# A two-block kernel on one Trainium2 core: the first block's mixer steps regrouped by ScalarE table set

## The reference, cut to what matters

```python
# gated delta rule: q, k, v are projected, convolved (4 taps) and passed through Silu
qkv = jax.nn.silu(causal_depthwise_conv(jnp.concatenate([q, k, v], axis=-1), conv_w))
q, k, v = jnp.split(qkv, 3, axis=-1)
q = l2norm(to_chunks(q, DN_HEADS, DN_DHEAD)) * (DN_DHEAD ** -0.5)
k = l2norm(to_chunks(k, DN_HEADS, DN_DHEAD))
M = jnp.where(strict, beta * (k @ k.T) * decay, 0.0)     # by chunk of 64 tokens
T = inverse(eye + M);  u0 = T @ (beta * v);  wk = T @ (beta * exp(G) * k)
qk = (q @ k.T) * decay
# a scan over the 8 chunks with u0, wk, qk, then per head:
o = rmsnorm(o, norm_g) * jax.nn.silu(z)

# HGRN2
fg = lb + (1.0 - lb) * jax.nn.sigmoid(f)
qc, kc, Bc = jax.nn.silu(q), 1.0 - fg, jnp.cumsum(jnp.log(fg))
# ... a scan over chunks, then:  o = rmsnorm(o, norm_g) * jax.nn.silu(g)

# second block, forgetting attention
fq = _rms(_to_heads(fx_q, FOX_HEADS)) * g_qk[0]
fk = _rms(_to_heads(fx_k, FOX_HEADS)) * g_qk[1]
```

## Time and profile before

| | |
|---|---|
| time, median of 3 runs | 3634.67 us (3631.44 to 3637.55) |
| the profiled execution: its own time | 3640.12 us |
| its span | 3638.4 us, TensorE's granted clock 0.985 of full |
| PE busy | 3562.5 us (98%) |
| VectorE busy | 1975.6 us (54%) |
| ScalarE busy | 1596.9 us (44%) |
| DMA | 368.21 MB, 101 GB/s |

### The profile page before, as it was taken

One profiled execution on the slowest core, in us unless ns is written; L12 is line 12 of the kernel. 1 busy time (PEld: TensorE's weight loads), 2 busy tenths in 40 slices (PEclk: granted clock), 3 DMA queues, 4 the chain that ended last, 5 costly groups with the idle time before them and its releaser, 6 DMA issues.

```text
span 3638.4 us, 50031 instructions
## 1 busy us (share of the span) xinstructions
PE 3562.5 (98%) x20724; PEld 2984.6 (82%) x20724; DVE 1975.6 (54%) x3335; ACT 1596.9 (44%) x2472; POOL 111.5 (3%) x202
## 2 busy tenths in 40 slices
PE   9999999999999999999999979999999999889999
PEld 7887988887887888898888758888888887678888
DVE  6966577548773677454445555444533345553332
ACT  7457444336655534242223694322332237843221
POOL 0000100010000100010000100000000000000000
PEclk9999999999999999999999999999999999999999
DMA  3101244431201244434443211444332321112232
GB/s 125 65 31 41 88 153 148 154 129 65 65 24 58 93 149 152 153 98 159 147 148 125 68 49 45 157 156 148 130 104 96 95 91 59 47 54 92 99 99 86
DMA packets 108690, 368.21 MB, mean 101 GB/s; under 512 B 14129, under 2 KB 16561, under 8 KB 108465
## 3 DMA queue, kind: packets, MB, share of 16 engines
q1 hardware_dynamic: 108464, 365.02, 30.1%
HBM read 360.78 MB, written 4.19 MB: 100 GB/s over the span
## 4 chain that ended last, share of the span: by engine, by line
PE 86%; ACT 7%; DVE 5%; issue 1%; POOL 0%; DMA 0%; SPq 0%; DVEq 0%; ACTq 0%; POOLq 0%
PE bank L175 84%; ACT L400 3%; ACT tmp L190 1%; PE bank L259 1%; DVE score L217 1%; DVE ast L214 1%; ACT wh L190 1%; PE bank L181 1%; DVE wl L193 1%; DVE tmp L196 0%; ACT lr L190 0%; ACT hh L190 0%; DVE dv L196 0%; ACT fl L190 0%; ACT lu L190 0%
## 5 line engine op out<-in xcount | busy, mean ns | idle before, releaser
L175 PE MATMUL bank<-hh,wh 128*128 128x512 f32 (+2 forms) x3424 | 1290.9, 377 | 18.3 <-ACT lg L190 13.0
L175 PE MATMUL bank<-hh,wl 128*128 128x512 f32 (+2 forms) x3424 | 1284.8, 375 | 0.7 <-DVE wl L193 0.7
L175 PE MATMUL bank<-hl,wh 128*128 128x512 f32 (+2 forms) x3424 | 1285.3, 375 | 0.0
L190 ACT ACTIVATE wh<-raw 128x1024 fp32r<-128x1024 f32 (+1 forms) x542 | 559.4, 1036 | 1449.0 <-PE bank L175 1443.8
L193 DVE TENSOR_TENSOR wl<-raw,wh 128x1024 fp32r<-128x1024 f32 (+1 forms) x542 | 646.7, 1196 | 843.1 <-ACT wh L190 842.9
L175 PEld LDWEIGHTS bank<-hh,wh 128*128 128x128 f32 (+1 forms) x3424 | 648.7, 189 | 138.7 <-issue 28.8
L175 PEld LDWEIGHTS bank<-hh,wl 128*128 128x128 f32 (+1 forms) x3424 | 648.2, 189 | 114.1 <-issue 5.6
L175 PEld LDWEIGHTS bank<-hl,wh 128*128 128x128 f32 (+1 forms) x3424 | 648.7, 189 | 111.8 <-issue 6.5
L175 PE MATMUL bank<-ah,wh 128*128 128x512 f32 (+1 forms) x1188 | 437.1, 368 | 0.0
L175 PE MATMUL bank<-ah,wl 128*128 128x512 f32 (+1 forms) x1188 | 437.0, 368 | 0.0
L175 PE MATMUL bank<-al,wh 128*128 128x512 f32 (+1 forms) x1188 | 436.4, 367 | 0.0
(11 more groups left out here) (353 smaller groups left out, 3551.6 us busy)
## 6 DMA issues: line engine op xcount, KB each, us to landing
raw<-in_up_dram SPq DMA_DIRECT2D x264, 512.0 KB, 3.3
raw<-in_ada_dram SPq DMA_DIRECT2D x144, 512.0 KB, 4.3
raw<-in_in_dram SPq DMA_DIRECT2D x88, 512.0 KB, 3.3
raw<-in_down_dram SPq DMA_DIRECT2D x96, 448.0 KB, 3.3
raw<-in_down_dram SPq DMA_DIRECT2D x48, 512.0 KB, 3.5
raw<-in_out_dram SPq DMA_DIRECT2D x32, 512.0 KB, 3.3
x<-in_x_dram SPq DMA_DIRECT2D x16, 256.0 KB, 5.2
raw<-in_in2v_dram SPq DMA_DIRECT2D x8, 512.0 KB, 3.5
```

Source lines behind the costliest of these rows:

```text
L175: s = self.put(lambda e: e.matmul(out, lhsT, rhs, **kw), records * max(records * n, 2 * m) / 2.4)
L190: return self.put(lambda e: e.activation(out, x, func, **kw), cost, tables)
```

## The change

Three things are edited. The Ln of `head_rstd` no longer asks for the set `natural_log`, so it takes the set that holds both Ln and Exp. `dn_project` is split into `conv` (project, taps, Silu) and `unit` (the norm), and runs k0 k1, their norms, then q0 q1 v0 v1, then the norms of q. `hg_project` runs the Sigmoids of both f tiles, then the Ln, scan and Exp of both, then the Silus of q0 q1 g0 g1. The planner's distance for a near step becomes a parameter; no section sets it, and its default is 5.2e3 where it was 4 x 1300.

```diff
-DEFAULT = dict(slack=(20e3, 100e3), part=0.5, more=3e3, stay=5e3, busy=20.0, goal=3.7e3)
+DEFAULT = dict(slack=(20e3, 100e3), part=0.5, more=3e3, stay=5e3, busy=20.0, goal=3.7e3, near=5.2e3)
...
-            near = [r for r in ready[e] if (not steps[r[1]].tables or table in steps[r[1]].tables) and r[0] < pick[0] + 4 * switch]
+            near = [r for r in ready[e] if (not steps[r[1]].tables or table in steps[r[1]].tables) and r[0] < pick[0] + way["near"]]
...
-    log = q.act.activation(t.ap[:, :], b.ap[:, :], ACT.Ln, bias=mem.eps[:, 0:1], scale=1.0 / n, table="natural_log").then_inc(q.act.sem, 1)
+    log = q.act.activation(t.ap[:, :], b.ap[:, :], ACT.Ln, bias=mem.eps[:, 0:1], scale=1.0 / n).then_inc(q.act.sem, 1)
...
     def dn_project(p):
         q, v, d = mem.lane("dn_in"), mem.pairs[p], {}
-        for kind, dst in enumerate((v.q, v.k, v.v)):
-            for e in range(2):
...
+        def conv(kind, e):
+            u = 4 * kind + 2 * p + e
+            b, done = project(u)
...
+            d[kind, e] = q.act.activation(y, y, ACT.Silu).then_inc(q.act.sem, 1)
+
+        def unit(kind, e):
+            y, t, b = to[kind][:, e, :], in_tmp.next(), prep.next()
+            m = sum_squares(mem, q, y, d[kind, e], mem.k("ones"), b, t)
...
+        for kinds, normal in (((1,), 1), ((0, 2), 0)):
+            for kind in kinds:
+                for e in range(2):
+                    conv(kind, e)
             for e in range(2):
...
+                unit(normal, e)
         return d
...
     def hg_project(wait):
-        q, d, tmp = mem.lane("hg_in"), {}, Turn(tmps[2:4])
-        for i in range(2):
-            b, done = project(22 + i)
-            q.act.wait_ge(done, wait)
-            d["q", i] = q.act.activation(mem.hq[:, i, :], b.ap[:, :], ACT.Silu).then_inc(q.act.sem, 1)
...
+        q, d, ts = mem.lane("hg_in"), {}, tmps[2:4]
+        for i, t in enumerate(ts):
             b, done = project(24 + i)
...
+        for i, t in enumerate(ts):
             rest, minus, least = (x[:, i:i + 1] for x in mem.bounds[l])
...
-            b, done = project(26 + i)
-            q.act.wait_ge(done, wait)
-            d["g", i] = q.act.activation(mem.hg[:, i, :], b.ap[:, :], ACT.Silu).then_inc(q.act.sem, 1)
...
+        for name, to, u in (("q", mem.hq, 22), ("g", mem.hg, 26)):
+            for i in range(2):
+                b, done = project(u + i)
+                q.act.wait_ge(done, wait)
+                d[name, i] = q.act.activation(to[:, i, :], b.ap[:, :], ACT.Silu).then_inc(q.act.sem, 1)
```

More of the change, by code:

```diff
@@ new lines, in dn_project @@
+        to = v.q, v.k, v.v
+        def conv(kind, e):
+            u = 4 * kind + 2 * p + e
+            b, done = project(u)
+            w = lambda k: mem.p1(l, "conv", 12 * k + u)
+            y = to[kind][:, e, :]
+            q.act.wait_ge(done)
+            s = q.act.activation(y, b.ap[:, :], ACT.Copy, scale=w(3)).then_inc(q.act.sem, 1)
+            for k in (2, 1, 0):
+                z = 3 - k
+                q.dve.wait_ge(s)
+                s = q.dve.scalar_tensor_tensor(to[kind][:, e, z:], b.ap[:, 0:S - z], w(k), to[kind][:, e, z:], ALU.mult, ALU.add).then_inc(q.dve.sem, 1)
+            b.free = [s]
+            q.act.wait_ge(s)
+            d[kind, e] = q.act.activation(y, y, ACT.Silu).then_inc(q.act.sem, 1)
@@ new lines, in unit @@
+        def unit(kind, e):
+            y, t, b = to[kind][:, e, :], in_tmp.next(), prep.next()
+            m = sum_squares(mem, q, y, d[kind, e], mem.k("ones"), b, t)
+            q.act.wait_ge(m)
+            log = q.act.activation(t.ap[:, :], b.ap[:, :], ACT.Ln, bias=mem.eps[:, 0:1]).then_inc(q.act.sem, 1)
+            b.free = [log]
+            q.act.wait_ge(log)
+            inverse = q.act.activation(t.ap[:, :], t.ap[:, :], ACT.Exp, scale=-0.5, bias=mem.eps[:, 1:2] if kind == 0 else None).then_inc(q.act.sem, 1)
+            q.dve.wait_ge(inverse, d[kind, e])
+            d[kind, e] = q.dve.tensor_tensor(y, y, t.ap[:, :], ALU.mult).then_inc(q.dve.sem, 1)
+            t.free = [d[kind, e]]
@@ L1838, in hg_project @@
     def hg_project(wait):
-        q, d, tmp = mem.lane("hg_in"), {}, Turn(tmps[2:4])
-        for i in range(2):
-            b, done = project(22 + i)
-            q.act.wait_ge(done, wait)
-            d["q", i] = q.act.activation(mem.hq[:, i, :], b.ap[:, :], ACT.Silu).then_inc(q.act.sem, 1)
-            b.free = [d["q", i]]
+        q, d, ts = mem.lane("hg_in"), {}, tmps[2:4]
+        for i, t in enumerate(ts):
             b, done = project(24 + i)
-            t = tmp.next()
             q.act.wait_ge(done, t.free, wait)
-            s = q.act.activation(t.ap[:, :], b.ap[:, :], ACT.Sigmoid).then_inc(q.act.sem, 1)
-            b.free = [s]
+            d["k", i] = q.act.activation(t.ap[:, :], b.ap[:, :], ACT.Sigmoid).then_inc(q.act.sem, 1)
+            b.free = [d["k", i]]
+        for i, t in enumerate(ts):
             rest, minus, least = (x[:, i:i + 1] for x in mem.bounds[l])
-            q.dve.wait_ge(s, mem.bounds_ready, wait)
+            q.dve.wait_ge(d["k", i], mem.bounds_ready, wait)
             d["k", i] = q.dve.tensor_scalar(mem.hk[:, i, :], t.ap[:, :], minus, rest, ALU.mult, ALU.add).then_inc(q.dve.sem, 1)
@@ L1862, in hg_project @@
             d["gl", i] = q.pool.memset(mem.hgl[:, i, 0:1], 0.0).then_inc(q.pool.sem, 1)
-            b, done = project(26 + i)
-            q.act.wait_ge(done, wait)
-            d["g", i] = q.act.activation(mem.hg[:, i, :], b.ap[:, :], ACT.Silu).then_inc(q.act.sem, 1)
-            b.free = [d["g", i]]
+        for name, to, u in (("q", mem.hq, 22), ("g", mem.hg, 26)):
[3 more added lines that the diff above has]
+                d[name, i] = q.act.activation(to[:, i, :], b.ap[:, :], ACT.Silu).then_inc(q.act.sem, 1)
+                b.free = [d[name, i]]
         d["i"] = []
```

## The result

The changed kernel takes 3613.9 us (median of 4 runs, 3613.7 to 3616.5), the kernel before 3633.1 (4 runs, the three above among them): a ratio of 0.9949, 95% interval 0.9932 to 0.9966. Run again later beside others it took 3614.4 us, ratio 0.9940 (0.9926 to 0.9953). So the change makes the kernel faster by half a per cent, some 19 us; 3620 was predicted.

A forecast was written before the change was run, and what follows sets the result against it. TensorE was taken as full in the first block's long stretches, leaving gains in the mixers' ends: -7.7, -4.5 and -2.0 make -14.2 us, 3620.5 against the median of 3634.67. Predicted 3620 us, range 3602 to 3643.

The forecast's parts named there:

- The bound: First block's long mixer stretches: TensorE is full, so fewer loads there gain 0; at most some 4 us.
- Number of loads: Whole kernel: table loads fall from 192 to about 125, by 39, 20 and 8 for the three edits.
- Layer 2's end: End of first block's layer 2 mixer: six loads go where TensorE waits for ScalarE, -7.7 us; bounds 0 and -15.3.
- VectorE's half of each head: Layer 2's end: named as what is late next after the loads, but with room, busy 12.01 of 24 us.
- rival 1: Mixers' ends: another wait takes the loads' place, or loads don't fall; nothing gained, 3633 us; chance 0.18.
- Layer 1's end: End of first block's layer 1 mixer: head norm loads go, TensorE gives back its filler, -4.5 us; bounds 0 and -5.6.
- Second block: Its mixers: 8 loads a layer go, hidden under TensorE; -2 us over both layers; bounds -9.6 and +2.6 a layer.
- The delta rule's loop: Second pair, first block: loop starts 25.4 us later as q comes later; 0 in both layers, bound +7 in layer 1.
- rival 2: Delta rule: v1 still projected late, so q's norm and loop wait; slower, 3645 us, if v1's Copy passes 1045; chance 0.14.
- the slack: Layer 2, second pair: 29.1 us between the loop's end and u0, which takes in the loop's delay.
- Rival 3: Full stretches and second block: TensorE less full than it looks, so shorter ScalarE chains pay there too; 3600 us; chance 0.14.

The follow-up runs named there:

- b1: The kernel before, unchanged, run for a second profile: span 3628.5 us, first block's mixer of layer 1 396.61 us at a granted clock of 1.00.
- again: The changed kernel itself, run once more for a further profile: 3614.4 us, ratio 0.9940 to the kernel before.
- e1: The kernel before with only the head norms' Ln moved to the set of Ln and Exp, planned anew: 3622.1 us, ratio 0.9969.
- e2: The kernel before with only the delta rule's projection regrouped: ratio 1.0002, 172 loads.
- e3: The kernel before with only the HGRN2 projection regrouped: ratio 1.0006, 183 loads.
- e5: The kernel before, every engine's list in its old order, loads worked out anew with head norms' Ln in the shared set: 3623.3 us, ratio 0.9970.
- e9: The changed kernel with only the second block's head norms on a set of their own again, planned for: 3619.6 us, ratio 0.9963 to the kernel before.
- e8: The changed kernel with the LRU's root by Ln and Exp and the second block's planner told to stay on a loaded set: 3609.0 us, ratio 0.9932.
- e6: The changed kernel in its own order, with a separate set loaded again for each head norm, unplanned: 3656.2 us, ratio 1.0054 to the kernel before.
- b2: The kernel before, unchanged, run for a third profile: first block's mixer of layer 1 400.42 us at a granted clock of 0.99.

## Why the prediction was right, point by point

The sum, -14.2, stands against -15.2 between two executions at like clock (b1 and `again`) and -19 by the medians. Part of that nearness is luck: the terms missed in both directions.

*The bound.* PE full in the first block's long stretches: right. (The 3% of the chain are a rounded share, so 109 us is no upper bound, as the prediction has it; 3.5% would be 127. Nothing rests on it.) Regrouping by itself gave 1.0002 and 1.0006. From the mixer's start to the last z Silu the changed kernel is 2.2 us shorter in layer 1 (284.4 in b1, 282.2) and 2.3 in layer 2 (308.6, 306.3); the term was 0, the bound -4.

*Number of loads.* 125 forecast, 124 found, by parts 39, 20 and 9 (e1, e2, e3) where 39, 20 and 8 were put; none stands between a head's Ln and Exp.

*Layer 2's end.* Forecast -7.7. The mixer gained 7.5 to 8.7, but the term itself was too large: last z Silu to out projection went from 22.6 us, at a clock of 0.85 in all three profiles of the kernel before, to 16.7 at 1.00 in the first profile of the changed kernel and 17.9 at 0.81 in `again`: -4.7 to -5.9. e5 has -5.05 for the six loads alone, at 0.91. What the step had set aside came up: "VectorE's half of each head" is what ScalarE now idles for (0.36 and 0.84 us above), and PE still waits for tmp from 1121 to 1138, where under 2 us were forecast:
```profile
PE bank L175 <- ACT tmp L190: 4.5, 2, 3.2
```
It fills 6.9 us where 7.8 stood in the kernel before from the z Silu on, not half. So rival 1's mechanism took 2 to 3 of the 7.7 us. The rest came from ahead of the end, 2.3 us, and from behind it, 0.5. The total was met by two misses of opposite sign.

*Layer 1's end.* Forecast -4.5, measured -4.9 at equal clock for the mixer, again not as put: the stretch ahead of the last z Silu gave 2.2 us, all that is behind it 2.7 (112.2 to 109.5). The step costed the end's filler, 4.5 us, as the gain. In the whole mixer the filler (tile spinner; length, busy PE) fell by 2.7, b1 first, then `again`:
```profile
39.07:435.68 396.61, 9.84 (x36) 6.15 (x35) 0.00 (x0) 1.00 0.17 57
```
```profile
39.28:430.96 391.68, 7.19 (x29) 4.71 (x27) 0.00 (x0) 1.00 0.18 58
```
That the regroupings by themselves may lengthen what is behind the Silu, and the head edit take that out again (3 us by the estimate above), is missing from the prediction.

*Second block.* Mis-sized: -2 forecast, 5.3 by the table, 5 by the medians of e9. What the step says of the cover held: the loads dropped in the old order gave 0.2 and 0.3 us against b1 (e5), under the 1 us a layer that it took. What it left out is the planner, which sees that the loads are gone and orders the stretch anew; e1, with the head edit alone, has the same 5.3 us. The bound of -9.6 a layer had it.

*The delta rule's loop.* Half right. The second pair of layer 2 in ScalarE's timeline of the changed kernel:
```profile
1007.77 0.69 ACT L190 ACTIVATE dv<-bank,small 128x512 f32<-128x512 f32 x1 [0.87 <-PE bank L175]
...
1028.55 0.60 ACT L190 ACTIVATE bMT<-bank 128x512 f32<-128x512 f32 x1 [0.79 <-PE bank L175]
...
1054.55 1.27 ACT L190 ACTIVATE bZ<-bB 64x512 f32<-64x512 f32 x2
...
1058.87 0.60 ACT L190 ACTIVATE du<-bank 128x512 f32<-128x512 f32 x1 [1.58 <-PE bank L175]
```
Against the earlier trace rows, and allowing for the mixer's start, 14.3 us earlier, the loop starts 13.8 us later (25.4 forecast) and ends 14.4 later: the pair's six Copies came within 47.4 us, 9.5 a step, not 12.7. Yet u0 comes 10.4 us earlier: v1 is in at 1007.77, no longer behind the loop. So rival 2 fell at its own point of decision: v1's Copy, later than 1045 in its case, came at 1008. The forecast's claim that the delay fits into the slack held, with 4.3 us left of 29.1. In layer 1, where the bound was +7, the loop ends 2.9 us later and u0 comes 10.8 earlier. Rival 3's sign, over 5 us less in 38 to 285 or in 2033 to 2206, did not show either: the first is 2.2 us shorter, and the whole second block's mixer of layer 1 1.8.

*What nothing foresaw:* +2.3 us in the feed-forward part behind layer 2, the same in both profiles of the changed kernel and in those of e8 and e9. The order alone does not explain it, since e6, in the changed order with more loads, has +0.4; the cause is open. And 5.4 us were taken off the sum for the profiled execution's distance from the median, without asking where they lay; by b1 and b2 they lay in layer 1 and in its clock.

## What to carry to other kernels

Price a table load by the chain that it stands in, not by its number: here 68 loads, 87 us of ScalarE, gave 19 us, 30 of them in full stretches gave 0 to 4, and the same kind of load put in without a plan cost 1.07 us each. Before a stage is read as won or lost, profile the kernel before twice and compare the granted clock of the stage. Where a planner writes the order, keep the lists as they are in one run and let it plan anew in another: in the second block the same dropped loads gave 0.5 us in the old order and 5 in the new. And lay two orders side by side up to the same piece of work, and edits in pairs as well as apart.

## What the runs showed of the hardware

TensorE's clock fell to half its rate at one place in one execution of the kernel before and not in another, on the same lists of instructions, with PE busy throughout. The kernel before, first profile, then b1 around the same point of the mixer:
```profile
390.00:400.00 10.00, 10.00 (x86) 10.00 (x85) 3.83 (x11) 4.93 (x13) 4.82 (x7) 0.97 0.00 0
400.00:410.00 10.00, 10.00 (x49) 10.00 (x49) 2.84 (x3) 2.69 (x7) 1.71 (x2) 0.52 0.32 107
```
```profile
382.00:392.00 10.00, 10.00 (x88) 10.00 (x87) 2.29 (x7) 3.76 (x12) 0.00 (x0) 1.00 0.23 77
392.00:402.00 10.00, 10.00 (x89) 10.00 (x88) 5.72 (x10) 6.31 (x14) 6.54 (x8) 1.00 0.17 55
```
0.52 is next to the lower of the two levels, 1.2 GHz; 49 matmuls pass in 10 us instead of 89, and the busy time, 10.00 of 10 before and during it, tells nothing of it. What let the clock fall there is left open.
